# Two weight sums split in one instruction, and the seventh product's two sums in one

## The reference

```
h = rmsnorm(x); z = h @ w_in                      # combined projection
A = sliding-window attention (window 128, sinks, relative bias)
B = mLSTM matrix memory, chunks of 64 tokens
x = x + [rmsnorm(A) || o * rmsnorm(B)] @ w_out
u = max(rmsnorm(x) @ w_up, 0);  x = x + (u * u) @ w_down     # 1024 -> 4096 -> 1024
y = rmsnorm(x)
```

## Time and profile before

| | |
|---|---|
| time, median of 3 runs | 2346.86 us (2346.73, 2346.86, 2352.06) |
| profiled execution, its own time | 2347.0 us |
| profiled execution, span | 2345.2 us |
| PE busy | 2300.8 us, 98% of the span, 14430 matmuls |
| DVE busy | 1665.1 us, 71%, 3597 instructions |
| ACT busy | 1104.1 us, 47%, 2110 instructions |
| granted PE clock | 0.997 of full speed, mean of the span |
| chain that ended last | PE 88%, DVE 8%, ACT 2% |

### The profile page before, as it was taken

One profiled execution on the slowest core, in us unless ns is written; L12 is line 12 of the kernel. 1 busy time (PEld: TensorE's weight loads), 2 busy tenths in 40 slices (PEclk: granted clock), 3 DMA queues, 4 the chain that ended last, 5 costly groups with the idle time before them and its releaser, 6 DMA issues.

```text
span 2345.2 us, 37363 instructions
## 1 busy us (share of the span) xinstructions
PE 2300.8 (98%) x14430; PEld 2040.1 (87%) x14430; DVE 1665.1 (71%) x3597; ACT 1104.1 (47%) x2110; POOL 94.6 (4%) x161
## 2 busy tenths in 40 slices
PE   9999999999999999999999999999999999999998
PEld 8987899888897898898998788999878878989986
DVE  4478877777368877777456887777755788776775
ACT  4445544445345644455333554444534545444433
POOL 3000000000000000000000220000110000000000
PEclk9999999999999999999999999999999999999999
DMA  6212333234511232334521232333444112222222
GB/s 196 81 46 80 99 99 102 96 100 152 167 56 54 73 100 95 103 99 144 159 81 37 62 94 96 108 99 101 160 123 135 43 53 82 91 90 82 90 81 77
DMA packets 176652, 227.93 MB, mean 97 GB/s; under 512 B 15507, under 2 KB 126708, under 8 KB 176460
## 3 DMA queue, kind: packets, MB, share of 16 engines
q1 hardware_dynamic: 162636, 192.63, 26.4%
q10 hardware_dynamic: 6448, 19.40, 2.3%
q0 software_dynamic: 7392, 13.52, 2.0%
HBM read 214.13 MB, written 12.60 MB: 97 GB/s over the span
## 4 chain that ended last, share of the span: by engine, by line
PE 88%; DVE 8%; ACT 2%; issue 1%; DVEq 0%; ACTq 0%
PE ps L2470 18%; PE ps L2472 18%; PE ps L2471 18%; PE ps L2987 8%; PE ps L2988 8%; PE ps L2989 8%; PE ps L2481 2%; PE ps L2615 2%; PE ps L2595 1%; DVE w_lo L1417 1%; DVE a_lo L1456 1%; PE ps L2604 1%; PE ps L2661 1%; PE ps L2664 1%; DVE x_all L1456 1%
## 5 line engine op out<-in xcount | busy, mean ns | idle before, releaser
L2470 PE MATMUL ps<-w_hi,u_all 128*128 128x512 f32 x1024 | 403.1, 394 | 1.4 <-DVE w_lo L1417 1.4
L2472 PE MATMUL ps<-w_hi,u_all 128*128 128x512 f32 x1024 | 404.2, 395 | 0.0
L2471 PE MATMUL ps<-w_lo,u_all 128*128 128x512 f32 x1024 | 400.2, 391 | 0.0
L1456 DVE TENSOR_TENSOR x<-x,ps 128x512 f32<-128x512 f32 (+1 forms) x288 | 196.3, 684 | 135.1 <-PE ps L2472 117.4
L866 ACT ACTIVATE w_hi<-PT 128x512 fp32r<-128x512 f32 x224 | 128.4, 621 | 340.4 <-PE ps L2472 237.1
L2470 PE MATMUL ps<-w_hi,a_hi 128*128 128x290 f32 (+1 forms) x768 | 262.0, 341 | 1.3 <-DVE x L1456 0.9
L2987 PE MATMUL ps<-a_hi,w_hi 128*128 128x256 f32 (+1 forms) x896 | 255.5, 285 | 1.4 <-DVE wide L1456 1.4
L2988 PE MATMUL ps<-a_lo,w_hi 128*128 128x256 f32 (+1 forms) x896 | 255.8, 285 | 0.0
L2989 PE MATMUL ps<-a_hi,w_lo 128*128 128x256 f32 (+1 forms) x896 | 255.2, 285 | 0.0
L2471 PE MATMUL ps<-w_lo,a_hi 128*128 128x290 f32 (+1 forms) x768 | 252.6, 329 | 0.0
L2472 PE MATMUL ps<-w_hi,a_lo 128*128 128x290 f32 (+1 forms) x768 | 252.4, 329 | 0.0
(11 more groups left out here) (427 smaller groups left out, 4904.8 us busy)
## 6 DMA issues: line engine op xcount, KB each, us to landing
w_raw<-in_w_up_dram SPq DMA_DIRECT2D x128, 512.0 KB, 4.0
w_raw<-in_w_down_dram SPq DMA_DIRECT2D x128, 512.0 KB, 3.5
w_raw<-in_w_out_dram SPq DMA_DIRECT2D x32, 512.0 KB, 3.5
w_raw<-in_w_in_dram SPq DMA_DIRECT2D x24, 580.0 KB, 4.7
w_raw<-in_w_in_dram SPq DMA_DIRECT2D x22, 512.0 KB, 3.8
w_raw<-in_w_in_dram SPq DMA_DIRECT2D x32, 256.0 KB, 3.0
x<-in_x_prompt_dram ACTq DMA_DIRECT2D x9, 512.0 KB, 5.9
bias<-bias_rows POOLq DMA_DIRECT2D x32, 128.0 KB, 3.5
```

What stands on the lines that cost most here:

```text
L1456: return eng.tensor_tensor(out, a, b, op)
L2470: eng.matmul(out, lh, rh, start=(k == ks[0]), stop=False)
L2471: eng.matmul(out, lh, rl, start=False, stop=False)
L2472: ins = eng.matmul(out, ll, rh, start=False, stop=(k == last))
```

## The change

S2 is now made right after S1, and S3 last, so that S1 and S2 lie side by side in `PT`, and S4 and S3 too (`form_src` maps the names to the places 1, 2, 4, 3). `high_pair` and `low_pair` split two forms in one instruction of 1024 elements where their two ring slots adjoin (`side_by_side`); where the pair straddles the ring's end they fall back to two of 512. Forms 2 and 3 (S1, S2) are one pair, forms 4 and 5 (S4, S3) the other. In `staging` the two sums r and h become one tile `hr` of twice 256, so that `take_sum` 4 adds the sixth bank's product m7, broadcast, to both in one instruction, in place of `take_sum` 4 and 5.

```diff
         def form_src(q, u, name):
             if name[0] == "S":
-                return PT[:, int(name[1]) - 1, :].rearrange("p (a b) -> p a b", b=P)
+                return PT[:, "1243".index(name[1]), :].rearrange("p (a b) -> p a b", b=P)
...
+        def side_by_side(u, f):
+            return (ring_at(u) + f) % RING < RING - 1
+
+        def pair_at(t, u, f):
+            s = (ring_at(u) + f) % RING
+            return t[:, s * FORM:(s + 2) * FORM]
+
+        def pair_src(f):
+            return PT[:, f - 2:f, :].rearrange("p n e -> p (n e)")
...
+            def high_pair(q, u, f):                       # ACT
+                if not side_by_side(u, f):
+                    high_form(q, u, f)
+                    high_form(q, u, f + 1)
+                    return
+                eng.wait_ge(f_sum.sem, f_sum.at(q, 4 * seven(u) + f))
+                ring_free(eng, q, u, f)
+                ring_free(eng, q, u, f + 1)
+                eng.activation(pair_at(w_hi_all, u, f), pair_src(f), ACT.Copy).then_inc(f_high.sem, 2)
...
-                        for f in ((0, 1), (2,), (3, 4), (5, 6))[n]:
+                        if n in (1, 2):
+                            high_pair(nq, nu, 2 * n)
+                            return
+                        for f in (0, 1) if n == 0 else (6,):
                             high_form(nq, nu, f)
...
                     tt(src("S1"), src("A21"), src("A22"), ALU.add).then_inc(f_sum.sem, 1)
-                    tt(src("S3"), src("A11"), src("A21"), ALU.subtract).then_inc(f_sum.sem, 1)
-                else:
                     eng.wait_ge(f_sum.sem, f_sum.at(q, 4 * at + 1))
                     tt(src("S2"), src("S1"), src("A11"), ALU.subtract).then_inc(f_sum.sem, 1)
-                    eng.wait_ge(f_sum.sem, f_sum.at(q, 4 * at + 3))
+                else:
+                    eng.wait_ge(f_sum.sem, f_sum.at(q, 4 * at + 2))
                     tt(src("S4"), src("A12"), src("S2"), ALU.subtract).then_inc(f_sum.sem, 1)
+                    tt(src("S3"), src("A11"), src("A21"), ALU.subtract).then_inc(f_sum.sem, 1)
...
+            def low_pair(q, u, f):                        # DVE
+                if not side_by_side(u, f):
+                    low_form(q, u, f)
+                    low_form(q, u, f + 1)
+                    return
+                eng.wait_ge(f_high.sem, f_high.at(q, 7 * seven(u) + f + 2))
+                tt(pair_at(w_lo_all, u, f), pair_src(f), pair_at(w_hi_all, u, f).bitcast(F32), ALU.subtract).then_inc(f_split.sem, 2)
...
-                        ins = tt(c_at[1][:, HT:TQ], m7[:, 0:HT], r6, ALU.add)
-                    elif n == 5:
-                        ins = tt(c_at[1][:, 0:HT], m7[:, 0:HT], h5, ALU.add)
+                        halves = lambda t: t.rearrange("p (n t) -> p n t", n=2)
+                        ins = tt(halves(c_at[1][:, 0:TQ]), m7[:, 0:HT].unsqueeze(1).broadcast_to([P, 2, HT]), halves(hr), ALU.add)
...
-                            for f in ((0, 1), (2, 3), (4,), (5, 6))[n - 2]:
+                            if n in (3, 4):
+                                low_pair(nq, nu, 2 * n - 4)
+                                return
+                            for f in (0, 1) if n == 2 else (6,):
                                 low_form(nq, nu, f)
```

More of the change, by code:

```diff
@@ L519, in staging @@
             at = 2 * T + ws
-            s1, r6, h5, s5 = (line[:, a:b] for a, b in ((2 * T, at), (at, at + HT), (at + HT, at + 2 * HT), (at + 2 * HT, at + 2 * HT + NS)))
-            return ws, c_at, s1, r6, h5, s5
+            s1, hr, s5 = (line[:, a:b] for a, b in ((2 * T, at), (at, at + 2 * HT), (at + 2 * HT, at + 2 * HT + NS)))
+            return ws, c_at, s1, hr, s5
         def x_flat(last):
@@ L861, in high_form @@
                 if name[0] == "S":
-                    eng.wait_ge(f_sum.sem, f_sum.at(q, 4 * seven(u) + {"S1": 1, "S3": 2, "S2": 3, "S4": 4}[name]))
+                    eng.wait_ge(f_sum.sem, f_sum.at(q, 4 * seven(u) + {"S1": 1, "S2": 2, "S4": 3, "S3": 4}[name]))
                 else:
@@ L1185, in quarter @@
                 high_tile(q, NT, NT - 1)
-                ws, c_at, s1, r6, h5, s5 = staging(last)
+                ws, c_at, s1, hr, s5 = staging(last)
                 def t_high_part(name):
@@ L2281, in take_sum @@
                         eng.wait_ge(m_done.sem, m_done.at(q, 7 * at + 4))
-                        ins = tt(r6, m6[:, 0:HT], s1[:, 0:HT], ALU.add)
+                        ins = tt(hr[:, HT:2 * HT], m6[:, 0:HT], s1[:, 0:HT], ALU.add)
                     elif n == 2:
@@ L2286, in take_sum @@
                             eng.tensor_copy(s5, m5[:, HT:ws])
-                        ins = tt(h5, m5[:, 0:HT], r6, ALU.add)
+                        ins = tt(hr[:, 0:HT], m5[:, 0:HT], hr[:, HT:2 * HT], ALU.add)
                     elif n == 3:
@@ L2290, in take_sum @@
                         eng.wait_ge(c_add.sem, c_add.at(q, 7 * at + 3))
-                        ins = tt(c_at[0][:, 0:HT], m3[:, 0:HT], h5, ALU.add)
+                        ins = tt(c_at[0][:, 0:HT], m3[:, 0:HT], hr[:, 0:HT], ALU.add)
                     elif n == 4:
@@ L2302, in take_sum @@
                             tt(c_at[1][:, TQ:TMAX], m4[:, HT:ws], s5, ALU.add)
-                        eng.wait_ge(c_add.sem, c_add.at(q, 7 * at + 5))
+                        eng.wait_ge(c_add.sem, c_add.at(q, 7 * at + 6))
                         ins = tt(c_at[1][:, HT:TQ], c_at[1][:, HT:TQ], m4[:, 0:HT], ALU.subtract)
-                    ins.then_inc(c_add.sem, 1)
+                    ins.then_inc(c_add.sem, 2 if n == 4 else 1)
                 def low_up(u, t, off, w, n):
@@ L2360, in step @@
                         take_sum(u, 4)
-                        take_sum(u, 5)
                         next_part(5)
```

## The result

The changed kernel takes 2352.64 us, median of 20 runs (2351.48 to 2355.13). The kernel before, timed beside it, takes 2349.74, median of 20 (2346.55 to 2352.27). The ratio is 1.0014 with a 95% interval of 1.0008 to 1.0020, so the change costs 0.14%. That is less than the 0.3% that the prediction took as the least difference that can be told, but with 20 against 20 runs the whole interval lies above 1, so it is a small loss. One run of the kernel before, 2861.16 us at a granted clock of 0.736, was slow and is left out of every comparison. The forecast was 2348.8 in a range to 2352.0; the time lies 0.64 above the range. The profiled execution took 2353.84 us, 6.8 more than the one of before.

What follows compares the result with a forecast made beforehand. The prediction took PE to bound the kernel, busy 2300.8 of 2345.2 us. Steady part 0, starts 0.6 + 0.5 and ends 0.8 made +1.9 on 2347.0, lying 0.14 above the median 2346.86: 2348.8 us, range 2345.0 to 2352.0.

Steps and rivals of the forecast that it cites:

- Steady part, 0: Steady part of each quarter's MLP: PE is busy throughout, so DVE's savings and the pair's later forms cost 0.
- (b): Rival: DVE paces more than the windows show and its savings reach the end, 2340.7 to 2322.5 us; chance 0.03.
- (c): Rival: in every steady unit DVE reaches `take_sum` 0 too late for the sixth product, 2373 us; chance 0.04.
- Savings: DVE's busy time, from merged pairs and the merged sum: falls by 15 to 24 us with the time unchanged.
- Starts, +1.1: First seven-product unit of each quarter: third product waits longer for the pair, 0.6 us over quarters 0 to 2, 0.5 in quarter 3.
- Ends, +0.8: End of quarters 0 to 2: loads into `PT` issue 1.5 to 1.6 us later, PE's wait grows 0.27 each.
- (a): Rival: savings reach PE at the quarters' starts and both waits there vanish, -3.2 us, 2343.7; chance 0.09.
- (d): Rival: the ring's fall-back is common or the pairs do nothing for the path, nothing moves, 2346.9 us; chance 0.20.
- the case that had 0.02: Remaining case at the quarters' ends: a delay of the loads near its bound, 1.6 us each, 4.8 in all; chance 0.02.

Runs made afterwards that it cites:

- e4: The kernel before with the seventh product's two sums merged into one instruction and no pairs: 2350.18 us, ratio 1.0005.
- e1: The changed kernel with forms 4 and 5 split one by one again in each quarter's last seven-product unit: 2349.68 us, ratio 1.0000 to the kernel before.
- e2: The changed kernel with all pairs, but the first two loads wait only for the forms that read their places in `PT`: 2349.60 us, ratio 1.0003 to the kernel before.
- e5: The changed kernel as it is, timed and profiled a second time: 2352.28 us, ratio 1.0015 to the kernel before.
- e6: The changed kernel with DVE's pair of forms 4 and 5 behind the last tile's take: 2352.49 us, ratio 1.0020 to the kernel before.
- e3: The kernel before, without the change, its first two loads also waiting for the third product of the last U unit: 2356.39 us, ratio 1.0038.

## Why the prediction was right and wrong

- **Steady part, 0: right.** PE is busy 255.00 of 255.00 us. DVE waits for ACT's pair, 3.32 us in the unit shown and 180.1 us in 48 waits over the whole kernel, 3.75 each (forecast some 3), and no product waits in the steady part. The rivals (b) and (c) fall.
- **Savings: right in kind.** DVE's busy time fell by 19.8 us (forecast 15 to 24) with nothing given to the time. The merged sum costs 691 ns, where I had taken 684; its saving of 0.156 us each was sized too large, since e4 shows 3.9 us for all 56, 0.07 each:

```profile
L1492 DVE TENSOR_TENSOR wide<-ps,wide 128x512 f32<-128x512 f32 x56 | 38.7, 691 | 26.2 <-issue 26.1
```

- **Starts, +1.1: too large, measured +0.57.** The wait before the third product came out as said (1.11 to 1.19, forecast 1.1 to 1.3), that before the sixth went to 0. In quarters 0 to 2 the sum per start is 1.11 to 1.19 against 1.06: +0.05 in quarter 0, +0.13 in quarters 1 and 2. The forecast was 0.16 to 0.2, taken as 0.2. The group on ACT that the merged split delays, in quarter 0 and in quarter 1, and DVE's two pairs:

```profile
254.48 0.60 ACT L1267 ACTIVATE wide<-ps 128x512 f32<-128x512 f32 x1 [1.33 <-PE ps L2509]
810.89 0.58 ACT L1267 ACTIVATE wide<-ps 128x512 f32<-128x512 f32 x1
257.05 2.35 DVE L1492 TENSOR_TENSOR w_lo<-PT,w_hi 128x1024 fp32r<-128x1024 f32 x2
```

In quarter 1 ACT's idle time before the group (1.03 us before the change) is used up and the 0.1 us that the prediction had left over passes on. In quarter 0 ACT still idles 1.33 us, so none of its delay passes on, and what is left is the pair's 1.22 in place of 0.69. But there PE had lost 1.7 us at the clock in the window at 230, which gave ACT that much more room. In e1, e2, e5 and e6, too, every start of 1.11 stands behind such a stretch, and every one of 1.15 or 1.17 behind none. In quarter 3 the wait was 0.26 for a forecast 0.5, since ACT's last group came 0.2 us later against PE and not 0.44.
- **Ends, +0.8: the step that failed, measured +5.64.** The prediction had the place, the 1.6 us of delay and the mechanism, and then let 1.3 of it go: "the next two start at 531.7 in place of 531.44 [...]: 0.27 us later". It followed the order of issues on ACT's queue. That part is there, 0.5 to 0.6 us of each end in place of 0.27. But the chain also waits for the data, which the prediction put at nothing: 4.04 of the 5.64 us. Between the second load's landing at 536.2 and ACT's square at 537.14 there were 0.9 us of slack, which the issue's 1.6 us overran; and the second load's flight grew, to 8.3 us from 6.5 in quarter 0, for a reason that stays open. Even the upper bound, 1.6 us for each or 4.8 in all, had left the flight out: the first end grew by 2.59, the second by 1.92, the third by 1.13. e2 took away the late issue and with it all of the loss; e3 put it into the kernel before and made it.
- **The time.** On profiles the forecast was +1.9, measured +6.8: 6.2 of waits, 1.2 of a longer warm-up (11.04 us against 9.87), -0.6 of rest; both lose 3.4 us at the clock. On the runs it was +2.9 at the medians, or 5.1 at equal clock. Of the 3.8 us by which 2352.64 lies above 2348.8, 2.9 are the base, 2346.86 from three runs against 2349.74 from twenty, and 1.0 the change. That the change shows so little of its 5.1 us is luck at the clock. Rivals (a) and (d) fall with the waits. What came is the case that had 0.02, a delay of the loads near its bound, or past it (5.64 against 4.8). The prediction's own bounds, +7.9 on 2346.86, reach 2354.8; the range stopped at 2352.0, where one of the three runs of before already stood (2352.06). A kernel whose runs fall in heaps 2 to 3 us apart wants a range that takes in the heaps.
- **The weighing of grouping against breaking up** (the Trainium skill, Perfetto Trace Analysis, Optimizing Scalar/DVE Operations). The traces bear out the second statement, on bubbles: DVE was not saturated (71%), grouping saved 19.8 us of its time, and the bubble on PE before the third product grew from 0.58 to 1.11 us, that at the end of quarter 0 from 0.43 to 3.02; e1, which breaks up that one pair again, brings it back to 0.45.

## What to carry to other kernels

A merged instruction waits for the later of the two inputs and hands over both results at its end; what it costs is read on the last thing that stands behind it on its engine, here the permission for a load. Where a load is made later, follow its data from issue to landing to the first reader, and look at what will now be in flight beside it. Before two medians are compared at 0.1%, look whether the runs of one kernel fall in heaps, and compare inside a heap.

## What the runs showed of the hardware

- The third and fourth of the four loads in the changed kernel, quarter 0 (KB each, median us to landing):

```profile
t_plain<-in_x_prompt_dram ACTq DMA_DIRECT2D x2, 512.0 KB, 11.0
```

- Four loads of 512 KB on one queue that go out right behind each other took 6.7 us (median of the first two) and 11.0 us (of the next two) in quarter 0, against 5.7 and 8.8 us with 2.2 us between the pairs, and 4.2 and 8.3 with 1.0 us between the first two and 1.8 to the next (e2). Loads of weights of the same size on SP's queue were in flight beside them in all three. At the end of quarter 2 the same spacing as in quarter 0 gave 5.8 us for the first two against 6.0 before.
- After a wait of PE of some 2 us the granted clock stood at half, its lower level of 1.2 GHz, for about 3.4 us in some executions (256 columns 0.21 us apart in place of 0.12), which costs 1.7 us each time; in others not, after the same wait in the same kernel. Near 1740 us it stood at half for 6.8 us, a loss of 3.4, behind 32-column matmuls and with no wait above 0.2 us ahead of it.
- The 72 warm-up matmuls at the start took 9.73 to 10.58 us in four profiles of one kernel, and 11.04 and 11.11 in two of the changed one.
- On DVE without pause two 1024-wide forms take 2.35 us (the row at 257.05), the second so 1.13, where four of 512 had taken 2.49: a merge saves 0.07 us.
